# Hybrid decoder block: the mixing stage's steps one deeper, recurrence products moved from GpSimd to VectorE

## The chip, the cores and the metric

One core of one Trainium2 chip (trn2). The metric is the device time of one execution in microseconds, here the median of three runs. One core has five engines that run side by side, each with its own queue in program order: TensorE (PE in the rows, its weight loads PEld), VectorE (DVE), ScalarE (ACT), GpSimd (POOL) and SyncE (SP, which here only issues transfers). They wait for one another by semaphores.

## The reference, cut to what matters

One sequence of 512 tokens, width 1024, float32. The stage that changes is the mixer, between an input projection and an output projection:

```python
proj = h @ w_in                                # 3584 columns: aq, ak, av | hq, hf, hi, hg
# four heads of differential attention (two softmaxes of 64-wide queries and keys each)
s = einsum(q, k) * scale; p = softmax(where(causal, s, -inf))
ao = rmsnorm((p[:, :, 0] - lam * p[:, :, 1]) @ v, g_diff_sub) * (1.0 - lam_init)
# four heads of HGRN2: S_t = diag(f_t) S_{t-1} + k_t v_t^T, o_t = S_t^T q_t, k = 1 - f
ho = rmsnorm(hgrn2(silu(hq), 1 - f, hi, log f), g_hgrn_out) * silu(hg)
y = concatenate([ao, ho]) @ w_out
```

Behind it come a norm, a residual and a product-key expert layer (16384 experts, top 16 of 8 heads), which the change does not touch.

## The kernel before, in words

The program is a row of stages, each a block that all engines leave together: `stage_project`, `stage_mix`, `stage_join`, then selection, gates and experts. The large matmuls split each float32 operand into a high and a low part (`PASSES`, three products each) and stream weights in units of 128 x 1024.

**Projection** (L383 to L606). 16 column units give `projT` (queries, keys and the recurrence's q and f, turned), then three groups of four row units give `projN` (av, hg, hi). TensorE is busy nearly all the time. Between units VectorE also multiplies the conditioning vector into `w_ada` (`ada_dve`, L300), a pair of chunks at a time, due at the units in `PAIR_UNIT`. The partial sums in `acc` are added over partitions by 32 small products with a column of ones (`sum_partitions`, L312), later, in the mixing stage. SyncE's queue loads units and pairs in one written order (L447 to L472).

**Mixing** (L624 to L1006). The order is written out by hand for each engine as steps n = 0 to 17; the steps 0 to 15 are one head and one block of 128 queries each, head n // 4 and block t = n % 4, which sees k = 128 (t + 1) keys. In step n:

- TensorE makes the scores of step n into banks 0 to 3 (L943, and the causal mask by L946), then `mixedT` times v of step n - 2 (L955), then four of the 32 sums of `acc` (steps 0 to 7) or the matmuls of two level units (steps 8 to 17, L930), then turns `mixed` of step n - 1 (L973), for which it waits on VectorE.
- VectorE takes the row maxima of step n (two L840, then L842), then combines the two softmaxes of step n - 1 into `mixed` (L850 to L854, which wait for ScalarE), then in steps 1, 3, 5, 7, 9 and 11 an item of the recurrence (a subtraction of 128 x 2048: L862, L866 or L875), and in steps 8 to 17 two masked copies (L830).
- ScalarE takes the exponentials of step n (L768, waiting for `mixed` of step n - 1, because `prob` has one buffer for the pair), then copies, squares, and the exponentials of the item (L788 to L800).
- GpSimd first builds the masks (L704 to L720), then multiplies the item's exponentials with q and k into F (L725 to L742), then the norm weights into hg (L743).

The recurrence inside a chunk of 128 tokens is a sum over five levels (`LEVELS`); a level has four heads, a head is one unit of four 128 x 128 matmuls, so there are 20 units, two to a step. The first product of levels 3 and 4 reuses F's slots.

When the steps are over, TensorE turns the last product (`kbT`, L982), multiplies it with hi (L990), VectorE carries the state (L894 to L900), and TensorE forms the output of the four blocks (L1001, L1004) in banks 4 to 7. Two norms follow: GpSimd multiplies the attention rows with inverse norm and weight (L749, L751); for the recurrence VectorE copies the bank to `cat` (L907), ScalarE squares it (L809), VectorE sums (L903), ScalarE takes one root for all blocks (L811), and VectorE and GpSimd multiply the rows by the inverse norm and by hg (L693, L695).

```python
                    if n >= 2:
                        pe.wait_ge(probs_ready, 2 * (n - 1))
...
                if 1 <= n <= STEPS_A:
                    o = n - 1
                    pe.wait_ge(mixed_ready, o + 1)
```

The first wait stands ahead of the scores of step n, the second ahead of TensorE's last work of step n.

**Join** (L1011 on) turns `cat` (L1197), copies each of its eight pieces (L1084) and takes the low part (L1131), then multiplies with `w_out` (L1189).

Of the kernel before, what the change touches and what calls it, by code (L numbers as in the profile page):

```python
# [5 lines left out]
F32 = mybir.dt.float32  # L6
# [7 lines left out]
P = 128  # L14
# [70 lines left out]
def build(nc, a):  # L85
    with ExitStack() as outer:
# [27 lines left out]
        m.rows = sb("rows", [P, TT, D])  # L114

# [115 lines left out]
def row_units_pe(nc, pe, m, hl, n0, e0, groups, piece_lo=None):  # L231


    def body(g, first):
        for u in range(RAW):
            pe.wait_ge(m.unit_lo, g * RAW + (n0 + 1 + u))
            if piece_lo is not None and first:
                pe.wait_ge(piece_lo, 2 * u + 2)
# [11 lines left out]
    with pe.Fori(1, groups) as g:  # L250
        body(g, False)
# [131 lines left out]
def stage_project(nc, a, m):  # L383
# [6 lines left out]
    m.lb = m.sb("lb", [P, 2, HEADS], F32, m.keep)  # L390
    m.ada_landed = [m.sem(f"ada_landed{i}") for i in range(ADA_SLOTS)]
# [6 lines left out]
    with ExitStack() as own:  # L398
# [28 lines left out]
        first_summed = m.sem("first_summed")  # L427
# [3 lines left out]
        def _(sp):  # L431
# [31 lines left out]
            sp.dma_start(m.small[:], a.small).then_inc(small_landed, 16)  # L463
            sp.wait_ge(m.ada_dved, 1)
# [11 lines left out]
        def _(pool):  # L476
# [8 lines left out]
            m.pool.then(pool, nc.gpsimd.memset(restart[:], 1.0))  # L485
            nc.gpsimd.memset(restart[:].rearrange("p (n c) -> p n c", c=CHUNK)[:, :, 0:1], 0.0
                             ).then_inc(restart_ready, 1)
# [38 lines left out]
        def _(dve):  # L526
# [37 lines left out]
            dve.wait_ge(small_landed, 16)  # L564
# [19 lines left out]
            dve.wait_ge(m.ada_dved, len(PAIRS_FIRST) + len(PAIRS_LATER))  # L584

        @block.tensor
        def _(pe):
# [16 lines left out]
            row_units_pe(nc, pe, m, hl, 16, 16, 3)  # L604
# [19 lines left out]
def stage_mix(nc, a, m):  # L624
    with ExitStack() as own:
# [19 lines left out]
        masks = sb("masks", [P, len(LEVELS), P])  # L645
        negmask = sb("negmask", [P, P], BF16)
# [10 lines left out]
        g_diff = small[:, 4 * QK + 2 * HEADS:4 * QK + 2 * HEADS + HD]  # L657
        g_hgrn = small[:, 4 * QK + 2 * HEADS + HD:]

        masks_ready = m.sem("masks_ready")  # L660
        mod_summed, mod_read = m.sem("mod_summed"), m.sem("mod_read")
        hg_ready = m.sem("hg_ready")
# [20 lines left out]
        hgrn_read = m.sem("hgrn_read")  # L683
        squares = m.sem("squares")
        sums = m.sem("sums")
        roots, inverses = m.sem("roots"), m.sem("inverse_norms")

        hgv = hg.rearrange("p (t n) -> p t n", t=TT)

        def norm_recurrence(engine, eng, step, t):  # L690

# [10 lines left out]
        def _(pool):  # L702
# [24 lines left out]
            for level in range(1, len(LEVELS)):  # L727
                h = LEVELS[level]
                pool.wait_ge(exp_ready, level + 1)
                if level == 3:  # L730
                    pool.wait_ge(level_done, HEADS)
# [1493 lines left out]
```

## Time and profile before

| | us |
|---|---|
| runs before: median of 3 (lowest, highest) | 1940.55 (1937.95, 1943.77) |
| the profiled execution: its own time | 1938.18 |
| its span, first to last instruction | 1936.5 |
| projection, to the last of L271 | 215.2 |
| mixing, first VectorE instruction to the end of L695 | 215.5 to 367.1 |
| join and what follows | 367.6 to 1936.5 |

PE is busy for 93% of the span, DVE for 61%, ACT for 36%, POOL for 34%; the mean granted clock of TensorE is 0.949 of 2.4 GHz. In a row of instructions the first number is the start or the place, then time in us, engine, line, operation, `output<-input`, shape and count; what stands in brackets is the idle time before it and what ended it. A matmul of float32 stands as two records, one per pass.

### The profile page before, as it was taken

Reading aid. Unit: us, or ns where it says so; the run is one execution under the profiler, and the core shown is the slowest. Engines: PE = TensorE matmul, PEld = TensorE weight load, DVE = VectorE, ACT = ScalarE, POOL = GpSimd, SP = SyncE. Lnnn points to the kernel's source line nnn. Section 1 sums busy time; section 2 is a strip of 40 time slices with the busy share of each in tenths; the row PEclk is TensorE's granted clock in tenths of the full one; section 3 lists DMA queues with packets and bytes.
Section 4 is the critical chain, followed back from the end, with each engine's and each line's share of the span. In section 5 each row is a group of like instructions: output and inputs, shape, how many; then the busy total and the mean of one; then the engine's idle time right before and its main releaser. Section 6 shows DMA issues by size and latency. Waiting matters only on the chain. (4 is left out here: it accounts for less than half of the span.)

```text
span 1936.5 us, 23196 instructions
## 1 busy us (share of the span) xinstructions
PE 1791.5 (93%) x8309; PEld 1483.0 (77%) x8309; DVE 1181.0 (61%) x2034; ACT 701.1 (36%) x1107; POOL 666.5 (34%) x500
## 2 busy tenths in 40 slices
PE   7999796788998689999998999999899999999996
PEld 7777564667777578888887888888688888888885
DVE  3767467755999844554453333333367877778876
ACT  2313342352232245555553222223233333333332
POOL 0000334502777532222221000000256776667750
PEclk8999767898999899999999999999899999999998
DMA  8553000322223234645657655555488988899885
GB/s 326 212 219 118 1 1 1 131 88 98 76 69 121 82 130 149 198 159 188 195 162 223 218 181 174 178 189 179 172 287 295 351 319 322 321 339 351 326 298 198
DMA packets 159708, 369.92 MB, mean 191 GB/s; under 512 B 16288, under 2 KB 78240, under 8 KB 156192
## 3 DMA queue, kind: packets, MB, share of 16 engines
q1 hardware_dynamic: 137120, 302.08, 44.9%
q0 software_dynamic: 22528, 67.19, 9.7%
q8 instruction: 20, 0.33, 0.1%
q14 instruction: 40, 0.33, 0.1%
HBM read 306.30 MB, written 62.91 MB: 191 GB/s over the span
## 5 line engine op out<-in xcount | busy, mean ns | idle before, releaser
L2158 PE MATMUL bank<-hl,actT 128*128 128x512 f32 x2304 | 525.9, 391 | 8.9 <-DVE actT L2098 8.9
L2158 PEld LDWEIGHTS bank<-hl,actT 128*128 128x128 f32 x2304 | 434.1, 189 | 100.7 <-DVE hl L2093 9.7
L1882 PE MATMUL bank<-actT,hl 128*128 128x512 f32 x1440 | 329.5, 392 | 7.1 <-DVE hl L1853 6.8
L1882 PEld LDWEIGHTS bank<-actT,hl 128*128 128x128 f32 x1440 | 272.0, 189 | 64.3 <-DVE hl L1853 7.0
L1738 PE MATMUL bank<-actT,hl 128*128 128x512 f32 x1152 | 275.0, 395 | 6.4 <-DVE hl L1697 6.4
L1738 PEld LDWEIGHTS bank<-actT,hl 128*128 128x128 f32 x1152 | 213.9, 189 | 48.7 <-DVE hl L1697 6.7
L1518 PE MATMUL bank<-actT,hl 128*128 128x512 f32 x864 | 213.9, 408 | 38.2 <-POOL hl L1364 27.0
L2055 ACT ACTIVATE hl<-v_raw 128x1024 fp32r<-128x1024 f32 x128 | 135.6, 1060 | 286.1 <-PE bank L2158 255.2
L2014 POOL DMA_INDIRECT rows<-in_v,own_index x65 | 81.7, 1257 | 424.7 <-POOLq L1778 352.2
L1518 PEld LDWEIGHTS bank<-actT,hl 128*128 128x128 f32 x864 | 168.1, 197 | 77.7 <-POOL hl L1364 17.2
L2093 DVE TENSOR_TENSOR hl<-v_raw,hl 128x1024 fp32r<-128x1024 f32 x128 | 156.9, 1226 | 91.7 <-ACT hl L2055 91.2
L2020 POOL DMA_INDIRECT own_act<-early_activations,own_at x128 | 177.5, 1387 | 39.1 <-issue 39.1
L1636 POOL TENSOR_TENSOR onehot<-first_hits,slotsT 128x512 f32<-128x512 bf16 x48 | 91.2, 1900 | 261.0 <-DVE first_hits L1704 261.0
L1862 DVE TENSOR_TENSOR kept_acts<-kept_acts,group_gates 128x384 f32<-128x384 f32 x60 | 33.5, 558 | 171.5 <-ACT kept_acts L1836 124.1
L1364 POOL TENSOR_TENSOR hl<-raw,hl 128x1024 fp32r<-128x1024 f32 x32 | 86.9, 2714 | 83.5 <-ACT hl L1384 83.5
L1665 ACT ACTIVATE onehot<-first_hits,slotsT 128x128 f32<-128x128 bf16 x192 | 85.1, 514 | 78.4 <-DVE first_hits L1704 78.4
L1697 DVE TENSOR_TENSOR hl<-raw,hl 128x1024 fp32r<-128x1024 f32 x48 | 58.8, 1226 | 88.2 <-ACT hl L1651 88.2
L1853 DVE TENSOR_TENSOR hl<-raw,hl 128x1024 fp32r<-128x1024 f32 x60 | 73.3, 1226 | 59.1 <-ACT hl L1827 59.1
L1836 ACT ACTIVATE kept_acts<-bank 128x512 f32<-128x512 f32 x60 | 35.9, 598 | 197.5 <-PE bank L1882 197.5
L2014 POOL DMA_INDIRECT raw<-in_v,own_index x63 | 77.1, 1223 | 59.5 <-DVE raw L2114 27.5
L1754 PEld LDWEIGHTS bank<-onehot 128*128 128x128 f32 x768 | 93.1, 191 | 3.7
L1754 PE MATMUL bank<-onehot 128*128 128x128 f32 x768 | 93.4, 275 | 0.0
(257 smaller groups left out, 2271.2 us busy)
## 6 DMA issues: line engine op xcount, KB each, us to landing
raw<-in_u SPq DMA_DIRECT2D x128, 512.0 KB, 3.8
v_raw<-in_v SPq DMA_DIRECT2D x128, 512.0 KB, 6.1
expert_gates<-gates SPq DMA_DIRECT2D x12, 2048.0 KB, 9.8
group_gates<-expert_gates SPq DMA_DIRECT2D x32, 768.0 KB, 5.9
acts_in<-early_activations SPq DMA_DIRECT2D x100, 192.0 KB, 5.0
wada<-in_w_ada SPq DMA_DIRECT2D x9, 2048.0 KB, 7.6
early_activations<-kept_acts SPq DMA_DIRECT2D x60, 256.0 KB, 2.1
early_activations<-gate_acts SPq DMA_DIRECT2D x48, 256.0 KB, 2.3
```

What stands on the lines that cost most here:

```text
L1364: g.tensor_tensor(hl[:, 1, u % m.split, :], raw[:, u, :], hl[:, 0, u % m.split, :].bitcast(F32), ALU.subtract).then_inc(m.unit_lo, 1)
L1518: last = nc.tensor.matmul(m.psum[u % 2][:], hl[:, x, u % m.split, kc * P:(kc + 1) * P], m.actT[:, z, kc, :], start=(kc == 0 and j == 0), s ...
L1636: nc.gpsimd.tensor_tensor(onehot1[:, b % BUFS, 0:pool_n, :].rearrange("p t k -> p k t"), hits[:, b % BUFS, :, 0:pool_n], slotsT[:, 2, n].u ...
L1665: last = A(onehot1[:, r % BUFS, u, :], hits[:, r % BUFS, :, u], ACT.Copy, scale=slotsT[:, 2, at:at + 1])
L1738: last = nc.tensor.matmul(m.psum[n % 2][:], hl[:, x, n % m.split, kc * P:(kc + 1) * P], m.actT[:, z, kc, :], start=(kc == 0 and j == 0), s ...
L1754: last = nc.tensor.matmul(chunk_bank(b, c)[:, k * NKEY:(k + 1) * NKEY], onehot1[:, b % BUFS, u, :], onehot2[:, b % BUFS, u, :], start=True ...
L1882: last = nc.tensor.matmul(m.psum[u % 2][:], hl[:, x, u % m.split, kc * P:(kc + 1) * P], m.actT[:, z, kc, :], start=(kc == 0 and j == 0), s ...
L2014: nc.gpsimd.indirect_dma_start(out=fetched[k % FETCH], out_offset=None, in_=rows_of_v, in_offset=bass.IndirectOffsetOnAxis(ap=m.own_index[ ...
L2020: nc.gpsimd.indirect_dma_start(out=own_act[:, k:k + 1], out_offset=None, in_=acts_of_u, in_offset=bass.IndirectOffsetOnAxis(ap=m.own_at[:, ...
L2055: A(v[:, 0, j, :], v_raw[:, j, :], ACT.Copy).then_inc(v_hi, 1)
L2093: V.tensor_tensor(v[:, 1, j, :], v_raw[:, j, :], v[:, 0, j, :].bitcast(F32), ALU.subtract).then_inc(v_lo, 1)
L2158: last = nc.tensor.matmul(bank(t, half)[:], w[:, x, j, t * P:(t + 1) * P], v[:, z, j, half * S:(half + 1) * S], start=(first and j == 0 an ...
```

## The change

It does the following.

1. **Steps one deeper.** `prob` has two buffers. ScalarE's exponentials of step n wait for `mixed` of step n - 2. TensorE turns `mixed` of step n - 2 and multiplies with v for step n - 3. There are 19 steps (0 to 18).
2. **Products on VectorE.** GpSimd keeps one memset in the stage. VectorE forms the products one step after the item, in steps 2, 4, 6, 8, 10, 12.
3. **Levels, states and outputs inside the steps.** Levels run in steps 4 to 13. The turned keys follow in steps 14 and 15, the products with hi in 15 to 17, states on VectorE in 15 to 17, and the outputs of blocks 0 to 2 in 17 and 18; they go to banks 0 to 3.
4. **Tail.** The copy to `cat` goes away: ScalarE squares from the bank, takes a root per block, and copies the bank to `cat` with the inverse norm as scale (four per block). VectorE multiplies with hg, and scales the attention rows by their inverse norm. All of it is interleaved block by block.
5. **Norm weights at the join.** `m.gsub` holds the two weight vectors as columns, loaded by two small transfers (128 partitions of 4 bytes each); ScalarE's copies of `catT` take it as scale, VectorE's low part becomes a scalar_tensor_tensor.
6. **Moved to the projection.** The masks are built by GpSimd in its first microseconds. TensorE's 32 sums stand between the units: 16 behind the column units, 8 behind row group 0, 8 behind row group 2; one VectorE addition follows.

Core of the diff:

```diff
-def row_units_pe(nc, pe, m, hl, n0, e0, groups, piece_lo=None):
+def row_units_pe(nc, pe, m, hl, n0, e0, groups, banks_free=True):
...
-                if u == 0 and not first:
+                if u == 0 and not (first and banks_free):
                     pe.wait_ge(m.unit_evac, g * TT + (e0 - TT + t + 1))
...
+            for i in range(2):
+                sp.dma_start(m.gsub[:, i:i + 1], a.small[0:1, at + i * HD:at + (i + 1) * HD].rearrange("o n -> n o")
+                             ).then_inc(small_landed, 16)
...
             row_units_dve(nc, dve, m, raw, hl, m.projN, 16, 16, 3, gates_of_recurrence, between=ada_pair)
             dve.wait_ge(m.ada_dved, len(PAIRS_FIRST) + len(PAIRS_LATER))
+            dve.wait_ge(mod_summed, 1)
+            nc.vector.tensor_tensor(m.mod[:, 16:48], m.psum[3][:, 0:32], m.bada[:, 16:48], ALU.add)
...
-            row_units_pe(nc, pe, m, hl, 16, 16, 3)
+            def sums_of_pairs(pairs):
+                pe.wait_ge(m.ada_dved, len(PAIRS_FIRST) + pairs[-1] + 1)
+                for i in pairs:
+                    for c in range(i * PAIR, (i + 1) * PAIR):
+                        last = sum_partitions(nc, m, m.psum[3][:, c:c + 1], acc[:, c, :])
+                return last
+            sums_of_pairs(range(0, 4))
+            row_units_pe(nc, pe, m, hl, 16, 16, 1)
+            sums_of_pairs(range(4, 6))
+            row_units_pe(nc, pe, m, hl, 20, 20, 2, False)
+            sums_of_pairs(range(6, 8)).then_inc(mod_summed, 1)
...
-LEVEL_AT = 8
+LAST = 3
+LEVEL_AT = 4
 LEVEL_END = LEVEL_AT + HEADS * len(LEVELS) // 2
 ITEMS = {1: 0, 3: 1, 5: 2, 7: 3, 9: 4, 11: "kb"}
+PRODUCTS = {2: 0, 4: 1, 6: 2, 8: 3, 10: 4, 12: "kb"}
+KB_AT = {14: (0, 1), 15: (2,)}
+KV_AT = {15: 0, 16: 1, 17: 2}
+OUT_AT = {17: (0,), 18: (1, 2)}
...
-        prob = sb("prob", [P, 2, S])
+        prob = sb("prob", [P, 2, 2, S])
...
-                    if n >= 1:
-                        act.wait_ge(mixed_ready, n)
+                    if n >= 2:
+                        act.wait_ge(mixed_ready, n - 1)
...
+            for t in range(TT - 1):
+                square_of_out(t)
+            root(0)
+            root(1)
+            scale_out(0)
+            root(2)
+            scale_out(1)
+            square_of_out(TT - 1)
+            scale_out(2)
+            root(TT - 1)
+            scale_out(TT - 1)
...
+            def products(level):
+                if level == 0:
+                    dve.wait_ge(exp_ready, 1)
+                    V.tensor_tensor(F[:, 0, :], E[:, 0, :], kk, ALU.mult).then_inc(f_ready, 1)
+                    V.tensor_tensor(F[:, 1, :], E[:, 1, :], q, ALU.mult).then_inc(f_ready, 1)
...
+                if n in KV_AT:
+                    carry(KV_AT[n])
+                if n in PRODUCTS:
+                    products(PRODUCTS[n])
                 item = ITEMS.get(n)
...
+            dve.wait_ge(attn_root, 1)
+            V.reciprocal(ss[:, 0], ss[:, 0]).then_inc(attn_inverse, 1)
+            dve.wait_ge(attn_inverse, 1)
+            attention_rows(0)
+            sum_squares(0)
+            attention_rows(1)
+            sum_squares(1)
+            sum_squares(2)
+            inverse(0)
+            inverse(1)
+            attention_rows(2)
+            inverse(2)
+            recurrence_rows(0)
+            attention_rows(3)
+            recurrence_rows(1)
+            sum_squares(TT - 1)
+            recurrence_rows(2)
+            inverse(TT - 1)
+            recurrence_rows(TT - 1)
...
+                for i in KB_AT.get(n, ()):
+                    turn_keys(i)
+                if n in KV_AT:
+                    keys_values(KV_AT[n])
+                for t in OUT_AT.get(n, ()):
+                    if t == 0:
+                        pe.wait_ge(probs_ready, 2 * STEPS_A)
+                    recurrence_out(t)
-                if 1 <= n <= STEPS_A:
-                    o = n - 1
+                if 2 <= n < STEPS_A + 2:
+                    o = n - 2
                     pe.wait_ge(mixed_ready, o + 1)
...
-                A(catT[:, 0, dc, :], m.psum[dc % 4][:], ACT.Copy).then_inc(cat_hi, 1)
+                A(catT[:, 0, dc, :], m.psum[dc % 4][:], ACT.Copy, scale=m.gsub[:, dc // HEADS:dc // HEADS + 1]
+                  ).then_inc(cat_hi, 1)
```

In the new order TensorE's level matmuls of step n still wait for the masked copies of step n - 1, which are VectorE's last work in that step.

## Rows read from the trace of the kernel before

**Rows 1.** Windows: us, busy PE, PEld, DVE, ACT, POOL (instructions), granted clock, DMA.

```profile
60.00:142.20 82.20, 80.21 (x355) 66.09 (x353) 55.97 (x72) 15.93 (x15) 0.00 (x0) 1.00 0.60 222
142.20:215.50 73.30, 66.82 (x288) 53.68 (x288) 44.98 (x54) 23.42 (x20) 0.03 (x1) 1.00 0.25 86
215.50:278.00 62.50, 52.20 (x168) 34.36 (x169) 35.87 (x68) 25.57 (x67) 25.47 (x25) 0.50 0.00 1
278.00:346.20 68.20, 48.52 (x266) 35.31 (x265) 50.28 (x75) 23.27 (x77) 24.13 (x7) 0.81 0.00 1
346.20:367.20 21.00, 11.81 (x102) 11.22 (x101) 17.06 (x23) 6.04 (x12) 12.97 (x10) 0.88 0.00 1
```

**Rows 2.** Waits, 215 to 368 us: who waited for whom, total, times, longest.

```profile
ACT prob L768 <- DVE mixed L854: 72.1, 14, 12.9
DVE nbias L840 <- PE bank L946: 36.5, 14, 5.2
PE bank L973 <- DVE mixed L854: 27.0, 8, 9.8
```

**Rows 3.** Timeline: VectorE beside a GpSimd product, and the same operation alone.

```profile
230.78 4.49 POOL L725 TENSOR_TENSOR F<-wada 128x2048 f32<-128x2048 f32 x1 [7.59 <-ACT wada L789]
230.86 4.70 DVE L854 SCALAR_TENSOR_TENSOR mixed<-prob,rz,mixed 128x256 f32<-128x256 f32 x1
...
264.80 0.48 DVE L854 SCALAR_TENSOR_TENSOR mixed<-prob,rz,mixed 128x256 f32<-128x256 f32 x1
```

**Rows 4.** Timeline: a step of VectorE beside no product, and a state product.

```profile
240.78 1.42 DVE L840 TENSOR_REDUCE nbias<-bank 128x1 f32<-128x512 f32 x2 [5.22 <-PE bank L946]
...
243.22 0.62 DVE L854 SCALAR_TENSOR_TENSOR mixed<-prob,rz,mixed 128x384 f32<-128x384 f32 x1
243.75 2.29 DVE L875 TENSOR_TENSOR wada<-projT 128x2048 f32<-128x2048 f32 x1
...
353.20 0.85 DVE L899 TENSOR_TENSOR state<-state,decay 128x512 f32<-128x512 f32 x1
```

**Rows 5.** Groups by form: count, busy us, mean ns, idle before.

```profile
L193 DVE TENSOR_TENSOR hl<-raw,hl 128x1024 fp32r<-128x1024 f32 x36 | 44.0, 1229 | 33.4 <-ACT hl L184 20.1 <-ACT hl L1072 10.7 <-ACT hl L500 2.5
L830 DVE COPY_PREDICATED attnT<-masks,bank 128x512 f32<-128x512 uint32 x20 | 14.0, 730 | 4.7 <-PE bank L930 4.7
L789 ACT ACTIVATE wada<-wada 128x2048 f32<-128x2048 f32 x1 | 1.9, 1909 | 0.0
```

**Rows 6.** Timeline: TensorE's scores (one of two), level units and values, at both clocks.

```profile
268.18 2.07 PE L943 MATMUL bank<-projT 64*128 64x512 f32 x2
...
277.59 3.23 PE L930 MATMUL bank<-F 128*128 128x128 f32 x16
...
283.62 1.95 PE L930 MATMUL bank<-F 128*128 128x128 f32 x16
...
316.88 0.91 PE L943 MATMUL bank<-projT 64*128 64x384 f32 x2
```

**Rows 7.** Windows, columns as in Rows 1: the granted clock around its changes.

```profile
274.00:278.00 4.00, 4.00 (x17) 3.10 (x16) 3.28 (x8) 3.94 (x10) 0.00 (x0) 0.50 0.00 0
278.00:282.00 4.00, 4.00 (x24) 3.44 (x22) 2.33 (x4) 1.81 (x9) 0.00 (x0) 0.71 0.00 0
322.00:326.00 4.00, 0.00 (x0) 0.00 (x0) 3.96 (x2) 0.00 (x0) 4.00 (x2) 0.83 0.00 0
354.00:358.00 4.00, 4.00 (x39) 4.00 (x38) 3.81 (x7) 1.71 (x3) 3.76 (x4) 1.00 0.01 4
```

**Rows 8.** Timeline: the sums at half clock, and gaps of TensorE between units.

```profile
142.19 22.05 PE L245 MATMUL bank<-hl,actT 128*128 128x512 f32 x96 [1.99 <-DVE hl L193]
165.02 5.76 PE L245 MATMUL bank<-hl,actT 128*128 128x512 f32 x24 [0.78 <-DVE projN L271]
217.91 1.81 PE L314 MATMUL bank<-ones,ada_sums 128*128 128x1 f32 x8
```

**Rows 9.** Timeline: the last VectorE instruction of the mixing stage.

```profile
366.43 0.69 DVE L695 TENSOR_TENSOR rows<-rows,projN 128x512 f32<-128x512 f32 x1
```

More of the change, by code:

```diff
@@ L249, in row_units_pe @@
     body(0, True)
-    with pe.Fori(1, groups) as g:
-        body(g, False)
+    if groups > 1:
+        with pe.Fori(1, groups) as g:
+            body(g, False)
 def row_units_dve(nc, dve, m, raw, hl, dst, n0, e0, groups, after=None, done=0, evac=None,
@@ L760, in _ @@
             A(lams[:, 2:4], lams[:, 0:2], ACT.Exp).then_inc(lam_exps, 1)
-            for n in range(STEPS_A + 2):
+            for n in range(STEPS_A + LAST):
                 if n < STEPS_A:
@@ L800, in _, with square_of_out, root, scale_out @@
                     A(e[:, :, h:], e[:, :, h:], ACT.Exp).then_inc(exp_ready, 1)
[L801 to L811 removed]
+                for i in KB_AT.get(n, ()):
+                    act.wait_ge(kb_tr, i + 1)
+                    A(kbT[:, i, :], m.psum[6 + i % 2][:], ACT.Copy).then_inc(kbT_ready, 1)
+            def square_of_out(t):
+                act.wait_ge(hgrn_out, t + 1)
+                A(E[:, 0, t * S:(t + 1) * S], m.psum[t][:], ACT.Square).then_inc(squares, 1)
+            def root(t):
+                act.wait_ge(sums, t + 1)
+                A(ss[:, 1, t, :], ss[:, 1, t, :], ACT.Sqrt, bias=m.eps[:, 0:1], scale=1.0 / HD).then_inc(roots, 1)
+            def scale_out(t):
+                act.wait_ge(inverses, t + 1)
+                for h in range(HEADS):
+                    last = A(cat[:, t, (HEADS + h) * HD:(HEADS + h + 1) * HD], m.psum[t][:, h * HD:(h + 1) * HD],
+                             ACT.Copy, scale=ss[:, 1, t, h:h + 1])
+                last.then_inc(scaled, 1)
+            A(ss[:, 0], ss[:, 0], ACT.Sqrt, bias=m.eps[:, 0:1], scale=1.0 / HD).then_inc(attn_root, 1)
+            for t in range(TT - 1):
[9 more added lines that the diff above has]
+            scale_out(TT - 1)
         @block.vector
@@ L932, in level_matmuls, with turn_keys, keys_values, recurrence_out @@
                     last.then_inc(level_done, 1)
-            for n in range(STEPS_A + 2):
+            def turn_keys(i):
+                if i == 0:
+                    pe.wait_ge(f_ready, 2 * len(LEVELS) + 2)
+                    pe.wait_ge(level_copied, HEADS * len(LEVELS))
+                if i >= 2:
+                    pe.wait_ge(kbT_ready, i - 1)
+                for h in range(HEADS):
+                    last = T.transpose(m.psum[6 + i % 2][:, h * HD:(h + 1) * HD],
+                                       F[:, 3, h * S + i * CHUNK:h * S + (i + 1) * CHUNK], m.ident[:])
+                last.then_inc(kb_tr, 1)
+            def keys_values(i):
+                pe.wait_ge(kbT_ready, min(i + 2, NCH - 1))
+                if i >= 2:
+                    pe.wait_ge(state_ready, i - 1)
+                for h in range(HEADS):
+                    last = T.matmul(m.psum[7 - i % 2][:, h * HD:(h + 1) * HD], kbT[:, i, h * HD:(h + 1) * HD],
+                                    hi[:, i, h * HD:(h + 1) * HD], start=True, stop=True)
+                last.then_inc(kv_done, 1)
+            def recurrence_out(t):
+                if t >= 1:
+                    pe.wait_ge(state_ready, t)
+                for h in range(HEADS):
+                    at = slice(h * S + t * CHUNK, h * S + (t + 1) * CHUNK)
+                    out = m.psum[t][:, h * HD:(h + 1) * HD]
+                    last = T.matmul(out, attnT[:, h, t * CHUNK:(t + 1) * CHUNK], hi[:, t, h * HD:(h + 1) * HD],
+                                    start=True, stop=(t == 0))
+                    if t >= 1:
+                        last = T.matmul(out, F[:, 2, at], state[:, t - 1, h * HD:(h + 1) * HD], start=False, stop=True)
+                last.then_inc(hgrn_out, 1)
+            for n in range(STEPS_A + LAST):
                 if n < STEPS_A:
```

265 lines of the change are left out of this document (95 added, 170 removed).

## The prediction

> **What bounds the kernel now.** I read the windows first [rows 1]. In the projection TensorE is busy for 80.2 of 82.2 us and 66.8 of 73.3 us, at full clock, so anything put into its queue there is paid, except in its gaps. In the mixing stage (215.5 to 367.1, 151.6 us) no engine is busy throughout: in its first 62.5 us VectorE works 35.9 us and TensorE runs at half clock; in the next 68.2 us VectorE works 50.3 us. The waits say why [rows 2]: VectorE stood 36.5 us ahead of its row maxima until TensorE had made the scores, TensorE stood 27.0 us ahead of its transposes until VectorE had made `mixed`, and ScalarE 72.1 us for the same. That is a ring: maxima, exponentials, `mixed`, transpose, scores of the next step. The engines take turns.
>
> A third loss hides in busy time. A combination of 128x256 that takes 0.48 us alone took 4.70 us, from 0.08 us behind the start of a 4.49 us GpSimd product and to its end [rows 3]. Nine instructions of VectorE (L842, L852, L854) are stretched so in the steps; each less its plain length (0.17, 0.35, 0.48), they lose 21.3 us. The Trainium skill ("SBUF — State Buffer", on the two sides of SBUF) says that VectorE with two SBUF inputs and GpSimd share a port pair, and that the loser blocks for the whole instruction; the trace agrees. Behind the mixing stage nothing changes but a few instructions of the join, so I leave all later stages at their times.
>
> **The change part by part.** S is the stage's first VectorE instruction; before, S is 215.5 and the stage ends at S+151.6.
>
> *VectorE's work.* A step without item costs, from the first maximum to the end of `mixed`, 3.06 us where the maxima are 512 wide [rows 4], and 2.45, 2.11 and 2.55 us for 128, 256 and 384; a group of four 10.2, sixteen 40.7. Six subtractions at 2.29 [rows 4] give 13.7. Twenty masked copies are 14.0 [rows 5]. New are the products: four of 128x2048 and eight of 128x1024. No such product ran on VectorE; the nearest row is its subtraction of two SBUF operands, 1.23 for 128x1024 [rows 5] and 2.29 for 128x2048, so 18.9. A state product of 128x512 with a broadcast took 0.85 [rows 4], which by size would give 27: that is the upper end; the lower is 18.9 itself. I take the nearer row. Three states are 3.8. Sum 91, against 86 us busy before (35.9 + 50.3): the products nearly fill what the contention leaves. So this part alone gives about 2 us; the gain must come from the 44 us that VectorE stood idle in 130.7 us of steps.
>
> *TensorE's work.* A group of four steps asks for scores (two 2.07 each plus the mask pieces for the widest, at half clock [rows 6]), values, transposes and eight level units (3.23 a pair at half clock, 1.95 at full [rows 6]). From the timeline that is 12.9 + 5.5 + 3.2 + 12.9 = 34.5 us at half clock, 8.6 a step; at full 7.4 + 3.1 + 1.8 + 7.8 = 20.1 us, 5.0 a step (the widest scores at full clock are scaled from the 384 ones, 0.91 a record pair). VectorE's level steps are 5.8, 6.4, 6.8, 6.3 us. So at full clock VectorE bounds the steps, at half clock TensorE does.
>
> *Opening, steps 0 to 4.* Scores 0 start with the stage; VectorE's `mixed` of step 0 ends at S+5.1, item 0 at 7.4, and ScalarE needs two exponentials of 1.91 [rows 5] until 11.2. VectorE has maxima 2 and `mixed` 1 until 10.0 and then waits 1.2; products to 15.8, step 3 to 21.1, step 4 with its copies to 27.5. The exponentials of step 2 stand behind item 0's on ScalarE, and the turned block 0 behind those, which holds TensorE from 8.9 to 12.9: in these steps I take its clock as low from S+9 on.
>
> *Level steps 5 to 13.* TensorE is now the fuller one and works without a gap from about S+20. Before, the clock rose at 278 to 282 after such a stretch, and fell only after it had been idle from 320 [rows 7]. I take it full from S+28 and kept, since the gaps at full clock are about 1.3 us a step. VectorE's work is 5.8 + 6.4 + 6.8 + 6.3 + 5.8 + 6.4 + 6.8 + 8.5 + 3.5 = 56.3; I add 0.5 for scores and for the last exponentials. End S+84.3. Scores of step n+1 need only TensorE's levels and transpose of step n, 1.95 + 0.5 us behind the copies, so they are there when VectorE asks.
>
> *Steps 14 to 18.* Here TensorE's queue sets the pace: scores 14 and 15, keys turned, kbT's copies on ScalarE behind its exponentials, three products with hi, and the values of 14 and 15. I walk 90.4 for scores 15, 95.5 for the last kbT, 101.0 for the last transpose, 102.8 for the last values, and 24 unit matmuls (48 records at about 0.11, since 39 records filled 4.00 us [rows 7], 5.4 us) to S+108.2.
>
> *Tail.* ScalarE: square, table load 1.28, root 0.3 to S+105.2. VectorE: 12 instructions at 0.69 and four short ones, with the waits on ScalarE's roots and its 1.1 us per scaled block: S+116.4. Before, from the last step to the end at 367.1 it was 20.9 us with one root for all [rows 1, 9]; now most of that stands beside TensorE's outputs. The stage: 151.6 - 116.4 = 35.2 us gained.
>
> *Paid back.* The 32 sums. At half clock eight records take 1.81 us [rows 8]; at full clock about 0.11 a record, so 16 sums are 3.5 us and 8 sums 1.8. They stand in gaps of 1.99 and 0.78 us [rows 8], which pays for part: +1.6, +1.0, and behind group 2 they run beside VectorE's copies, +0.2 for the addition. Sum +2.8. Bounds: 0 if later gaps take it up, +9 if a record costs 0.22 at full clock too. Their partial sums are ready: the pairs are due at units 10, 16 and 22 and asked for behind units 15, 19 and 27. Two column loads of tiny pieces pass SyncE's queue before a pair and unit 4, which is issued at 45 us and needed well behind 60: about 1 us, covered; if it were not, it is 1 us. The masks (6 us of GpSimd) go to 4 to 10 us, where VectorE starts at 13.3: nothing. Join: eight scalar_tensor_tensor for eight subtractions, 0.75 against 0.69: 0.5 us. The weights themselves leave GpSimd and cost nothing in a copy's scale.
>
> *Sum.* -35.2 + 2.8 + 0.5 = -32 on the profiled execution's 1938.2 us, so 1906. That execution lies 2.4 us under the median of the three runs; on the median it is 1908.
>
> **A rule that speaks against it.** VectorE becomes the bound of the level steps. The Trainium skill ("Perfetto Trace Analysis", optimizing Scalar/DVE operations) says that with VectorE saturated some work may be offloaded, even to GpSimd, but warns of their shared port. By the first half, keeping the products on GpSimd would spare 18.9 us; the rows price it at 21.3 us of blocking, so I go by the rows.
>
> **The rivals.**
>
> *Clock low in the level steps* (0.13). TensorE is short of work at full clock, has small gaps in every step, and the clock was 0.5 over the whole 62.5 us of [rows 1] although it was busy 52.2. Then steps 6 to 13 go at TensorE's 8.6: 69 us where I have 51, +18: 1926. Against it: it rose in the first level steps before. The Trainium skill ("TensorE: Matmul & The Clock Gate", the second failure mode) says that micro-idles between groups of matmuls let the clock oscillate; that is this case.
>
> *The overlap is partial* (0.13). The queues are in order, and the level matmuls still wait for the copies at the end of VectorE's step. If each of some 14 steps keeps 0.7 us of waiting, it is +10: 1918. This is also the case in which the deepening does not do what it says.
>
> *More than that* (0.08). TensorE now works until just before the barrier, so its clock may stay full through the opening, and steps 3 to 5 shrink by up to 7 us: 1901.
>
> *Slower or no change* (0.06 together). Half clock for the whole stage with TensorE as the only bound: 86.4 + 32.3 us in the steps, 18.7 for keys, states and outputs, some 10 of tail, 2.8 in the projection, sum 150, plus each gap in its queue. With 1.5 us of gaps it is 1938, no change; from 7 us of gaps on it is slower by over 0.3%, and with 15 us 1952. Before, it waited 27.0 for `mixed` alone [rows 2], so such gaps are real, but the clock did rise three times.
>
> **How the numbers follow.** Forecast 0.60 at 1908, then 0.13 at 1926, 0.13 at 1918, 0.08 at 1901, 0.03 no change, 0.03 slower. 0.3% (5.8 us) is about what a measurement of this kernel can tell. All but the last rival are faster by over that: 0.94, 0.03, 0.03. The range takes in 1901 with half of the clock's uncertainty below it, and the first two rivals: 1897 to 1926; the products' upper end (+8) and the sums' (+6) lie in it.
>
> **What would show it.** Right: the stage ends near S+116; L854's successor never over 0.8 us; VectorE idle in steps 6 to 13 under 1 us each; granted clock 1.0 from S+30 to S+108. Wrong: idle time ahead of the maxima of over 1 us a step with TensorE as releaser, 128x1024 products well over 1.3 us, a clock of 0.5 in the level steps, or the projection longer by over 5 us.

## The result, and the profile after

The changed kernel takes 1907.79 us (median of 4 runs, 1904.27 to 1910.94) where the kernel before takes 1940.9 beside it: ratio 0.9838, 95% interval 0.9823 to 0.9853. It is faster, within 0.3 us of the forecast. The profiled execution's own time is 1909.68, its span 1908.0, and TensorE's mean granted clock 0.959.

Windows of the changed kernel, columns as in Rows 1: the projection's second half, then the mixing stage from its start S = 218.5 to its last output of TensorE at 324.6 (its tail runs on to 331.7), then the start of the join.

```profile
145.50:218.50 73.00, 69.29 (x317) 57.12 (x316) 42.05 (x51) 23.41 (x20) 0.02 (x1) 0.99 0.21 75
218.50:246.00 27.50, 22.56 (x70) 12.40 (x70) 22.41 (x42) 14.22 (x35) 1.78 (x1) 0.57 0.00 1
246.00:304.50 58.50, 47.90 (x275) 35.73 (x276) 53.60 (x99) 27.74 (x81) 0.00 (x0) 0.88 0.00 1
304.50:324.60 20.10, 16.75 (x125) 13.91 (x123) 11.92 (x27) 12.01 (x37) 0.00 (x0) 1.00 0.00 1
332.00:341.20 9.20, 5.79 (x33) 5.50 (x33) 5.07 (x6) 6.04 (x9) 8.94 (x15) 0.69 0.90 344
```

VectorE is now busy for 53.6 of the 58.5 us of the level steps, where TensorE works 47.9: it bounds them. The stage takes 113.2 us against 151.6 [rows 1]: 38.4 gained.

Waits, 218 to 332 us, and groups of VectorE by form:

```profile
PE bank L1025 <- ACT mixedT L760: 10.0, 8, 3.6
...
PE bank L968 <- DVE attnT L829: 8.6, 6, 3.0
DVE nbias L874 <- PE bank L1016: 5.6, 4, 1.8
...
L829 DVE COPY_PREDICATED attnT<-masks,bank 128x512 f32<-128x512 uint32 x20 | 13.5, 725 | 0.6 <-PE bank L968 0.6
L853 DVE TENSOR_TENSOR F<-wada 128x1024 f32<-128x1024 f32 x4 | 4.9, 1219 | 0.0
L854 DVE TENSOR_TENSOR F<-wada,projT 128x1024 f32<-128x1024 f32 x4 | 4.9, 1218 | 0.0
L888 DVE SCALAR_TENSOR_TENSOR mixed<-prob,rz,mixed 128x512 f32<-128x512 f32 x4 | 3.0, 751 | 0.1
L837 DVE TENSOR_TENSOR F<-wada 128x2048 f32<-128x2048 f32 x1 | 2.3, 2293 | 1.4 <-ACT wada L769 1.4
L888 DVE SCALAR_TENSOR_TENSOR mixed<-prob,rz,mixed 128x256 f32<-128x256 f32 x4 | 1.9, 484 | 0.1
```

The 36.5 us ahead of the row maxima [rows 2] are 5.6. TensorE waits no longer for `mixed` but for ScalarE's copies of the turned block, 10.0 us, and for the masked copies, 8.6 us. The 128x256 combination that took 4.70 us [rows 3] takes 0.48 in the mean, and the products cost what the nearest rows said.

Timeline of TensorE: the 32 sums (two records each) in the projection, and the first instruction of the stage.

```profile
140.08 3.64 PE L314 MATMUL bank<-ones,ada_sums 128*128 128x1 f32 x32
...
167.03 1.84 PE L314 MATMUL bank<-ones,ada_sums 128*128 128x1 f32 x16
...
215.43 1.84 PE L314 MATMUL bank<-ones,ada_sums 128*128 128x1 f32 x16
218.52 0.64 PE L1013 MATMUL bank<-projT 64*128 64x128 f32 x2 [1.25 <-PEq L400]
```

The stage starts 3.0 us later than before. The records of the sums themselves are short (3.64 us for 32), but right behind the first 32 the granted clock was low for 3.4 us, with TensorE busy:

```profile
143.60:147.00 3.40, 3.40 (x9) 2.72 (x10) 3.22 (x6) 0.00 (x0) 0.00 (x0) 0.50 0.71 265
```

Behind the stage the join runs from 333.1 to 406.8, 73.7 us against 70.0 before. The stages behind the join start 31 to 32 us earlier than before; the experts' phase is 3 us longer in this execution, and 0.2 us longer than before in the second one below, so that belongs to the execution.

### The profile page after: what moved, and what is told of

The parts are those of the page before. It is cut to its first block and busy times, and to the rows that moved or that the text cites. A ratio compares the mean times of both kernels' runs of the same rounds, so it can differ in the third digit from the quotient of the medians.

```text
span 1908.0 us, 23185 instructions
## 1 busy us (share of the span) xinstructions
PE 1775.7 (93%) x8309; PEld 1473.8 (77%) x8309; DVE 1171.4 (61%) x2047; ACT 706.1 (37%) x1126; POOL 619.2 (32%) x477
## 5 line engine op out<-in xcount | busy, mean ns | idle before, releaser
L2057 POOL DMA_INDIRECT rows<-in_v,own_index x65 | 89.8, 1382 | 419.7 <-POOLq L1821 351.9
```

The source lines that it names most:

```text
L2057: nc.gpsimd.indirect_dma_start(out=fetched[k % FETCH], out_offset=None, in_=rows_of_v, in_offset=bass.IndirectOffsetOnAxis(ap=m.own_index[ ...
```

## The experiments

Each time stands against runs of the kernel before on the same chip. "Stage" is the mixing stage in the run's own profile, from its first to its last instruction on VectorE and ScalarE. It is one execution each: the same changed kernel gave 113.2 and 121.6, so a difference of some us between two stages can be of the execution. The rounds were made on different chips, so the changed kernel is compared with others by ratio too; its two rows are called its first and second series.

| run | time (lowest, highest) | ratio, 95% interval | stage |
|---|---|---|---|
| changed kernel | 1907.79 (1904.27, 1910.94) | 0.9838, 0.9823 to 0.9853 | 113.2 |
| changed kernel again | 1905.38 (1896.95, 1913.55) | 0.9815, 0.9791 to 0.9840 | 121.6 |
| before + deeper steps | 1923.19 (1921.73, 1924.17) | 0.9933, 0.9916 to 0.9949 | 138.4 |
| before + products on VectorE | 1922.13 (1919.83, 1924.39) | 0.9929, 0.9913 to 0.9946 | 134.4 |
| before + both | 1923.36 (1918.8, 1926.55) | 0.9917, 0.9899 to 0.9936 | 133.1 |
| changed, products on GpSimd | 1913.19 (1908.76, 1913.66) | 0.9872, 0.9855 to 0.9888 | 123.3 |
| changed, steps not deeper | 1908.53 (1906.43, 1912.8) | 0.9862, 0.9846 to 0.9879 | 115.9 |
| changed, levels late | 1911.27 (1908.22, 1915.18) | 0.9857, 0.9832 to 0.9882 | 115.3 |
| changed, old tail | 1908.86 (1903.53, 1912.51) | 0.9844, 0.9826 to 0.9863 | 115.0 |
| changed, sums twice | 1912.04 (1910.16, 1919.64) | 0.9863, 0.9841 to 0.9885 | 116.9 |
| changed, steps filled | 1900.88 (1899.44, 1902.46) | 0.9806, 0.9783 to 0.9830 | 110.6 |
| changed, sums fill the steps | 1899.74 (1896.61, 1907.54) | 0.9802, 0.9777 to 0.9827 | 114.4 |
| all together | 1900.21 (1896.56, 1901.8) | 0.9798, 0.9774 to 0.9822 | 113.4 |

**Products on VectorE, in the kernel before.**

```diff
+PRODUCTS = {2: 0, 4: 1, 6: 2, 10: 3, 11: 4, 14: "kb"}
...
-            g.tensor_tensor(F[:, 0, :], E[:, 0, :], kk, ALU.mult).then_inc(f_ready, 1)
...
+                    V.tensor_tensor(F[:, 0, :], E[:, 0, :], kk, ALU.mult).then_inc(f_ready, 1)
```

> The kernel before, with the recurrence products alone moved from GpSimd to VectorE (steps 2, 4, 6, 10, 11, 14; the norm weights stay on GpSimd). Theory 1 (the ring of turns between VectorE and TensorE is the loss, the contention nearly pays for the products): 21.3 us of stretching go, 18.9 us of products come, so -2 us, between -6 and +3. Theory 2 (the blocked port is the main loss and the products find room in idle time): -12 to -21 us.

14.4 us faster at the medians, inside the second theory's range and far outside the first's; the stage is 17.2 shorter. Waits and one group of this run, 215 to 352 us:

```profile
ACT prob L751 <- DVE mixed L859: 50.9, 14, 8.5
DVE nbias L845 <- PE bank L953: 19.6, 12, 3.5
PE bank L980 <- DVE mixed L859: 8.5, 10, 1.6
...
L837 DVE TENSOR_TENSOR F<-wada 128x1024 f32<-128x1024 f32 x4 | 4.9, 1218 | 0.0
```

VectorE's waits for the scores fell from 36.5 to 19.6 us, TensorE's for `mixed` from 27.0 to 8.5, with the ring as shallow as before. The products stand behind `mixed`, just where VectorE would wait for TensorE's transpose and scores: 18.9 us of work went into idle time of 36.5. So what the move takes away (the stretching) is gained, and what it adds is mostly not paid.

**Deeper steps, in the kernel before.**

```diff
-        prob = sb("prob", [P, 2, S])
+        prob = sb("prob", [P, 2, 2, S])
...
-                    if n >= 1:
-                        act.wait_ge(mixed_ready, n)
+                    if n >= 2:
+                        act.wait_ge(mixed_ready, n - 1)
```

> The kernel before, with the deeper steps alone (two buffers of prob, transposes of n - 2, values of n - 3, 19 steps); products on GpSimd, sums in steps 0 to 7, levels in 8 to 17. Theory 1: the 36.5 us that VectorE waited for scores shrink, but steps 0 to 7 stay bound by TensorE at half clock with the sums in them (58 us of work in 61 us), so -12 us, between -8 and -20. Theory 2: the blocked port stays, so -5 us or less.

13.3 us faster, as the first theory has it. The stretching stays; groups of VectorE:

```profile
L843 DVE TENSOR_SCALAR nbias<-nbias 128x2 f32<-128x2 f32 x16 | 12.5, 784 | 0.6
L855 DVE SCALAR_TENSOR_TENSOR mixed<-prob,rz,mixed 128x256 f32<-128x256 f32 x4 | 8.0, 2002 | 0.1
```

The scaling of two numbers a row, 0.17 us alone, takes 0.78 in the mean: eleven of the sixteen are plain, the longest takes 4.27.

**Both, in the kernel before.**

> The kernel before with both the deeper steps and the products on VectorE, and nothing else of the change. Alone they gave 13.3 and 14.4 us. First theory: both fill the same idle time of VectorE ahead of its maxima, so together they give what the products give plus the 3 to 5 us that the depth was worth in the changed kernel: 17 to 20 us, and VectorE's waits for the scores fall from 19.6 us to under 10. Rival: the deeper steps cut a chain of TensorE that the products leave alone, so the two add up to 25 to 28 us and the moved levels, states, outputs and the tail are worth only 5.

Neither 17 to 20 nor 25 to 28: 15.3 us at the medians, and the stage only 1.3 us shorter than with the products alone. VectorE's waits for the scores are 14.8 us, not under 10. The two edits cover largely one and the same idle time. That leaves 19.9 us of stage, down to 113.2, which neither explains; the levels' run below finds most of them.

**The changed kernel with the products on GpSimd.** GpSimd gets the body of before; nothing else moves.

> The kernel after, with the products back on GpSimd, each as soon as its exponentials are there. Theory 1: VectorE is the bound of the steps; it loses 18.9 us of products and gets about 22 us of blocking back, and a level may come late for its step: +5 us against the kernel after (0 to +9). Theory 2 (the skill's rule that a saturated VectorE is helped by moving work to GpSimd): -5 to -15 us against the kernel after.

As the first theory has it: 1913.19, a ratio 0.0034 over the changed kernel's (6.6 us), and the intervals do not meet. The stage is 10 longer than in the first profile of the changed kernel and 1.7 longer than in the second. One VectorE group:

```profile
L881 DVE TENSOR_SCALAR nbias<-nbias 128x2 f32<-128x2 f32 x16 | 11.5, 718 | 0.5
```

The stretching is back. Eleven instructions in the stage are longer than the same forms in the changed kernel, by 25.8 us in all; that is more than the 18.9 us of products that VectorE is spared, and the 6.9 between them are about what the kernel lost. The Trainium skill ("Perfetto Trace Analysis", optimizing Scalar/DVE operations) allows offloading from a saturated VectorE and warns of the shared port; here the warning decides, by 6.6 us.

**The changed kernel with steps not deeper.** One `prob` buffer, exponentials of step n wait for `mixed` of n - 1, transposes one step earlier.

> The kernel after, with the steps back to the depth of before (one buffer pair of prob, transposes of n - 1, values of n - 2, 18 steps). Theory 1: the ring is back, VectorE waits for the scores again, 1.5 to 2 us a step: +25 us against the kernel after (+15 to +32). Theory 2: it hardly matters once the products are off GpSimd: +5 us or less.

The rival was right, 5 us or less: the ratio is 0.0024 higher (4.7 us, with intervals that overlap; the medians differ by 0.7), the stage 2.7 us longer than in the first profile. TensorE waits 13.5 us for `mixed` and ScalarE 45.1, but VectorE, which bounds, only 10.5 for the scores (5.6 with the deeper steps):

```profile
ACT prob L747 <- DVE mixed L887: 45.1, 14, 6.3
PE bank L1043 <- DVE mixed L887: 13.5, 10, 2.2
DVE nbias L873 <- PE bank L1015: 10.5, 7, 3.0
```

**The changed kernel again.**

> The changed kernel itself, as the base of the runs beside it. Both theories expect 0.984 of the kernel before (0.982 to 0.9855), a mixing stage of about 113 us, and a join of 66 us with the granted clock low at its first products. If the 3 us by which the experts' phase was longer in its first profile are of that execution alone, they are not seen again.

The time agrees (the ratio lies 0.0005 under the expected range, the interval reaches into it), and the experts' phase is not longer again. But the stage of this profiled execution is 121.6 us, 8.4 longer than in the first. Up to the last copies the two are alike within 1.2 us. Then, windows of this run:

```profile
294.00:302.00 8.00, 4.93 (x26) 4.75 (x25) 7.13 (x13) 1.20 (x6) 0.00 (x0) 0.69 0.00 0
302.00:310.00 8.00, 8.00 (x26) 5.08 (x25) 2.71 (x8) 2.54 (x10) 0.00 (x0) 0.50 0.00 0
```

and of the first profile of the changed kernel, whose stage starts 0.4 us later:

```profile
294.00:302.00 8.00, 5.03 (x24) 4.26 (x23) 6.71 (x13) 1.96 (x8) 0.00 (x0) 0.59 0.00 0
302.00:310.00 8.00, 7.38 (x44) 4.78 (x43) 4.68 (x13) 3.81 (x15) 0.00 (x0) 1.00 0.00 0
```

The clock fell in the same step in both. TensorE had waited 0.6, 1.7 and 0.8 us between its matmuls and then waited some 3 us for the copies of step 12 (3.07 here, 2.97 there). Here the fall, at 297.1, lies in that wait. In the first profile it came at 293.7, 0.4 us ahead of it, so the wait of 3 us can't be its cause there; a window of the first profile:

```profile
293.00:294.00 1.00, 0.95 (x6) 0.74 (x6) 1.00 (x2) 0.28 (x2) 0.00 (x0) 0.87 0.00 0
```

What differs more is how long it stayed low: from 293.7 to 300.6 in the first, here from 297.1 to 310.7, into the steps where TensorE sets the pace and busy almost throughout, and again from 317.6 to 324.4. VectorE, with 4.68 us of work in 302 to 310 there, has 2.71 here: it waits. Timeline of TensorE of this run:

```profile
297.78 3.76 PE L968 MATMUL bank<-F 128*128 128x128 f32 x16 [3.07 <-DVE attnT L829]
...
302.32 1.65 PE L1013 MATMUL bank<-projT 64*128 64x384 f32 x2
```

**Old tail.** All from the last output's copy on as before; outputs of blocks 0 to 2 stay in the steps.

> The changed kernel with the tail of before behind its last output: VectorE copies every block to cat, one root for all blocks, GpSimd scales the attention rows and multiplies the last block. Outputs of blocks 0 to 2 stay inside the steps. First theory: the tail by blocks is worth what one root behind the fourth copy costs, 3 to 8 us, seen as a longer time from the last output product (now 7 us before the stage's end) to the stage's end. Rival: the gain at the end of the stage came from forming the outputs inside the steps, and the order of the tail is worth under 2 us.

1908.86: 3.5 us over the changed kernel's second series and 1.1 over its first at the medians, with intervals that overlap. From the last output product to the stage's end it takes 9.1 us instead of 7.2. That is the rival's price, under 2 us; the time alone does not decide. In its timeline VectorE and GpSimd again work at once, and a multiplication of 128x512 takes 1.6 us where the others take 0.69:

```profile
327.61 1.63 DVE L731 TENSOR_TENSOR rows<-rows,ss 128x512 f32<-128x512 f32 x1
329.27 0.69 DVE L733 TENSOR_TENSOR rows<-rows,projN 128x512 f32<-128x512 f32 x1
```

**Levels late.**

```diff
-LEVEL_AT = 4
+LEVEL_AT = 8
-PRODUCTS = {2: 0, 4: 1, 6: 2, 8: 3, 10: 4, 12: "kb"}
-KB_AT = {14: (0, 1), 15: (2,)}
-KV_AT = {15: 0, 16: 1, 17: 2}
-OUT_AT = {17: (0,), 18: (1, 2)}
+PRODUCTS = {2: 0, 4: 1, 6: 2, 10: 3, 11: 4, 14: "kb"}
+KB_AT = {18: (0, 1), 19: (2,)}
+KV_AT = {19: 0, 20: 1, 21: 2}
+OUT_AT = {20: (0,), 21: (1, 2)}
```

> The changed kernel with its levels in steps 8 to 17 instead of 4 to 13, the products of levels 3, 4 and of the keys at steps 10, 11 and 14, and the turned keys, states and outputs of blocks 0 to 2 behind the attention steps (18 to 21). Depth, products, tail and sums stay as changed. The kernel before with depth and products alone kept 15 us of the change's 33 to 36, the tail's order 6. First theory: what is left is mostly the place of the levels, so that keys, states and outputs run beside attention steps: a mixing stage 9 to 14 us longer than the changed one, time 0.987 to 0.990 of before. Rival: the place of the levels is worth under 5 us, and the rest is spread over masks, sums and the opening: 0.982 to 0.9845.

1911.27, ratio 0.9857: between the two ranges, and 5.9 us over the changed kernel's second series at the medians. Its stage is 2.1 us over the first profile of the changed kernel and 6.3 under the second, so the place of the levels is worth a few us, as the rival has it, and not 9 to 14. What it is good for is the comparison with "before + both", which has the same levels, depth and products but a stage of 133.1 us. The last `mixed` ends 11.8 us earlier here, measured from the first maximum, and what follows is 5.8 us shorter. Of the 11.8, 2.7 are there by step 5's maxima, 9.2 by step 7's and 9.9 by step 15's. TensorE's timeline of "before + both", step 1:

```profile
218.48 1.81 PE L314 MATMUL bank<-ones,ada_sums 128*128 128x1 f32 x8
220.22 1.22 PE L951 MATMUL bank<-projT 64*128 64x256 f32 x2
```

Eight such groups of sums stand in steps 0 to 7, at half clock, between scores that VectorE waits for; with the levels late they are gone from there. The clock rose earlier too: at 247.1 us with the levels late, at 269.6 in "before + both". The same window of the two, first of "before + both":

```profile
247.00:254.00 7.00, 7.00 (x24) 4.40 (x24) 3.77 (x6) 4.18 (x10) 0.00 (x0) 0.50 0.00 0
...
247.00:254.00 7.00, 6.45 (x29) 3.21 (x28) 6.83 (x11) 4.58 (x13) 0.00 (x0) 0.99 0.00 0
```

So most of the 9.2 us came between the maxima of steps 5 and 7, where one ran at half clock and the other mostly at full. How much is the sums' own time and how much the later rise was not taken apart. The masks, which GpSimd no longer builds in these microseconds, left with them and were not tried apart.

**Sums twice.** A second `sum_partitions` ahead of each.

> The changed kernel with each of the 32 sums between the projection's units done twice, so 64 more records on TensorE and the same result. First theory (a record costs 0.11 us at full clock, 0.23 a sum, and the gaps of the queue are already full): +5 to +7.5 us, the whole of 7.4. Rival: the projection's gaps between units cover part of it (they stood at 1.99 and 0.78 us before), so under 4 us. If it is the first, the 32 sums of the change cost about what the projection is longer by, 3 us, and half of them were covered.

The time is 6.7 us longer at the medians, in the first theory's range (by ratio 4.8 us over the first series, 9.3 over the second). In the profiled execution, the slowest of the five (7.6 us over their median), the sums cost more than expected where they were put: the projection ends 11.2 us later. TensorE's timeline of this run, and windows of it:

```profile
139.73 10.48 PE L314 MATMUL bank<-ones,ada_sums 128*128 128x1 f32 x64
...
225.28 3.86 PE L314 MATMUL bank<-ones,ada_sums 128*128 128x1 f32 x32
```

```profile
140.00:144.00 4.00, 4.00 (x35) 4.00 (x34) 3.96 (x7) 1.04 (x1) 0.00 (x0) 0.90 0.29 79
144.00:148.00 4.00, 4.00 (x21) 4.00 (x20) 3.82 (x6) 0.00 (x0) 0.00 (x0) 0.50 0.58 187
148.00:152.00 4.00, 4.00 (x16) 3.61 (x16) 0.89 (x2) 0.00 (x0) 0.00 (x0) 0.50 0.00 0
```

The first 64 records took 10.48 us and not 7.3, because the clock fell to 0.50 among them though TensorE was busy throughout, and the matmuls behind them paid as well. The last 32 took 3.86, the 0.12 a record that was expected.

**Steps filled.**

```diff
+FILL_AT = {7: 4, 8: 6, 11: 2, 12: 6, 13: 11}
...
+                if n in FILL_AT:
+                    pe.wait_ge(attn_read, n - 3)
+                    for i in range(FILL_AT[n]):
+                        T.matmul(m.psum[5][:, HD:HD + P], m.ident[:], m.ident[:], start=True, stop=True)
```

> The changed kernel with 29 idle matmuls of 128x128 on TensorE (a quarter of a us each at full clock) in steps 7, 8, 11, 12 and 13, where it otherwise stands 1.1 to 3.1 us for VectorE's copies and where its granted clock fell. Output as before. In two profiled executions of the changed kernel the clock came back after 6 us in one (stage 113.2 us) and after 16 us in the other (stage 121.6 us). First theory: the falls come with these idle stretches and are the changed kernel's spread; filled, the clock stays at 1.00 from 30 us to 105 us behind the stage's start, the stage takes 110 to 114 us, and the time is 3 to 5 us under the changed kernel's (0.979 to 0.981) with less spread. Rival: the clock falls anyway, or the idle matmuls delay scores and values as much as they save: 0.982 to 0.985.

The clock is as the first theory has it. Windows of the level steps and of the last steps, and TensorE's timeline at the place where the clock fell before:

```profile
240.00:295.00 55.00, 49.45 (x324) 37.96 (x324) 52.91 (x91) 27.77 (x82) 0.00 (x0) 0.99 0.00 1
295.00:320.00 25.00, 21.52 (x156) 17.35 (x154) 15.80 (x37) 14.12 (x45) 0.00 (x0) 1.00 0.01 1
```

```profile
289.61 2.72 PE L1022 MATMUL bank<-ident 128*128 128x128 f32 x22 [0.42 <-ACT rows L755]
292.17 0.83 PE L1030 MATMUL bank<-projN,mixedT 128*128 128x128 f32 x6
294.00 2.02 PE L969 MATMUL bank<-F 128*128 128x128 f32 x16 [1.00 <-DVE attnT L830]
```

The clock does not fall, the wait is 1.00 us instead of 3, the level matmuls take 2.02 instead of 3.76. The stage is 110.6 us, the time 4.5 us under the changed kernel's at the medians, and five runs lie within 3.0 us where six of the changed kernel span 16.6. Against the changed kernel's second series the ratio is only 0.0009 lower (1.7 us), against its first 0.0032 (6.2 us), and its interval overlaps with both. So the 4.5 is less certain than what the clock did.

**Sums fill the steps.**

```diff
+SUMS_AT = {7: (0, 4), 8: (4, 11), 11: (11, 13), 12: (13, 20), 13: (20, 32)}
...
+                if n in SUMS_AT:
+                    pe.wait_ge(attn_read, n - 3)
+                    for c in range(*SUMS_AT[n]):
+                        sum_partitions(nc, m, m.psum[5][:, HD + c:HD + c + 1], m.acc[:, c, :])
```

> The changed kernel with its 32 sums taken out of the projection and put where the run beside it has idle matmuls: 4, 7, 2, 7 and 12 of them ahead of the values of steps 7, 8, 11, 12 and 13; the addition of mod stands in VectorE's tail. First theory: the projection ends 3 us earlier, and the sums fill TensorE's idle stretches and hold the clock, as idle matmuls would: 4 to 8 us under the changed kernel, 0.9775 to 0.9805. Rival: the sums save their 3 us in the projection but their 0.11 us records do not hold the clock: 1 to 3 us, 0.980 to 0.982.

The time is the first theory's, the trace is the rival's. The stage starts at 213.8 us (216.4 to 218.5 in seven runs with the sums in the projection) but takes 114.4. The clock fell at each of the five groups of sums: 0.1 to 0.7 us behind the end of four, and within the last one; TensorE's timeline and two windows of it:

```profile
288.50 4.01 PE L314 MATMUL bank<-ones,ada_sums 128*128 128x1 f32 x24
```

```profile
286.00:290.00 4.00, 4.00 (x27) 3.10 (x27) 3.81 (x2) 1.80 (x9) 0.00 (x0) 0.93 0.00 0
290.00:294.00 4.00, 4.00 (x19) 4.00 (x20) 3.56 (x10) 1.02 (x4) 0.00 (x0) 0.50 0.01 2
```

**All together.**

> The version meant to be best: the sums filled into the steps as in the run beside it, the table of the square root loaded at step 16 by a root of a constant on ScalarE (1.28 us out of the chain of the tail), and 32 idle matmuls behind the last output, so that TensorE comes to the join without standing idle. First theory: the first less 1.3 us for the table and 1.8 us for the join's first products, which then go at full clock from their start: 0.976 to 0.979. Rival: the join waits for the first tiles of w_out and for ScalarE, and the clock falls there anyway: no better than the run without the two.

The rival: no better than its neighbour (0.9798 against 0.9802). The table does load at 310.9 us, out of the chain, and the idle matmuls do keep the clock up to the join. But the stage is only 1.0 us shorter, and the join takes 71.8 us against 70.1: its last transposes stand 2.85 us for VectorE's low parts instead. These last three versions are the fastest seen, at about 1900, though their intervals overlap with that of the changed kernel's second series.

## Why the prediction came out

**The walk held, place by place.** In the first profile the opening ended at S+28.4 (walked 27.5), the last masked copy at S+83.0 (84.3), the last values at S+100.6 (102.8), the last output at S+106.0 (108.2), the stage at S+113.2 (116.4). The kinds of term in it held too: products 1.22 and 2.29, the state product 0.69 and not 0.85, copies 0.73, wait for the exponentials 1.4 ahead of the first product (1.2). VectorE bounds the level steps, and its waits for scores in steps 5 to 13 are near nothing. The sum was -32 from -35.2, +2.8 and +0.5; the trace has -38.4, +3.0 and +3.7, so -31.7. The experts' +3.1 leaves 28.5 between the two profiled executions; the medians differ by 33.1. That the sum is met so closely is luck in part: the stage gained 3.2 us more than walked and the join lost 3.2 more than priced. And the walk met one execution of two; in the other the stage took 121.6 us against its 116.4.

**"So this part alone gives about 2 us" was wrong.** It set 21.3 us of stretching out against 18.9 us of products in, as if VectorE were the bound of the old steps too, in the same sentence that names its 44 us of idle time. Alone the move gives 14.4. And "the gain must come from" the idle time, which I tied to the deeper ring: the depth alone gives 13.3, but in the changed kernel it is worth 2.7 us of stage, and with the products already moved 1.3. The end points of the walk were right because a walk counts work and waits together; the shares given to the parts were not.

**One gain was not named.** The sums stand in the sum as a cost of 2.8 us only. What their leaving gives the opening (with the masks, and with the clock that rose earlier) is most of 11.8 us of stage, the second largest piece, against 3.0 paid in the projection. The walk had it by not listing them among TensorE's work.

**The sums' price of 2.8 came out at 3.0, but not for its reasons.** Behind the first 16 sums the next unit starts 1.4 us later than before (priced at 1.6). Then came the 3.4 us at half clock, which the forecast had at full: 1.6 more. The second group added 0.8 (priced at 1.0), and later gaps took back 0.7.

The stage by parts, in one order, each from single executions and so good to some us at best: products 17.2, depth 1.3, up to the last `mixed` (the sums and masks out of the opening, mostly) 11.8, the rest of the tail and outputs 5.8 (with rounding 17.8 for the two), levels early 2.1 in an execution whose clock fell briefly. In another order depth would stand first with 13.2.

**The clock: forecast and first rival are both partly true.** "I take it full from S+28 and kept" was wrong: it fell twice in the level steps, at 263.0 within a wait of TensorE of 1.7 us, and at 293.7 behind waits of 0.6, 1.7 and 0.8 us. What failed is the reading that the clock "fell only after it had been idle from 320": in the trace of before the clock had already fallen in the level steps, at 293.9, within a wait of 6.7 us, and stayed low to 304.2. That kernel's rows, a window and a timeline row of TensorE:

```profile
294.00:298.00 4.00, 1.27 (x3) 0.79 (x4) 3.88 (x4) 1.24 (x5) 2.39 (x2) 0.50 0.00 0
...
296.73 0.69 PE L973 MATMUL bank<-ident,mixed 128*128 128x128 f32 x2 [6.71 <-DVE mixed L854]
```

The walk came out in spite of it, because VectorE bounds most of those steps and a slower TensorE cost little (VectorE waits 0.3 us for scores in steps 5 to 13, and 1.7 ahead of the maxima of step 14). The rival priced it at +18 us for all of steps 6 to 13. Against the 110.6 us of the filled run, the stage is 2.6 us longer in one execution and 11.0 in the other. The Trainium skill ("TensorE: Matmul & The Clock Gate", the second failure mode) speaks of micro-idles that let the clock oscillate; the trace agrees, with falls among waits of 0.6 to 3.1 us, and filling five of them kept the clock at 1.00 from S+25 to S+107.

**The partial overlap** did not come: VectorE waits 5.6 us in all, 1.8 of it in step 1. TensorE is the one that waits, for ScalarE's copies (10.0 us) and for the masked ones (8.6 us).

**The join** was taken at +0.5 and came at +3.7. The code is not what it lost by: with the same join the run with the sums in the steps and the one with the sums twice took 70.1 us, before it was 70.0. (A copy with the weight as its scale takes 0.69 us instead of 0.60, so it is not free as forecast, but these two runs show no loss by it.) In the first profile of the changed kernel the first tile of `w_out` came later: ScalarE waited for it, then VectorE for ScalarE, then the last transposes 3.41 us for VectorE (1.10 before). ScalarE's timeline there, and in the run with the sums in the steps, whose join starts 3.5 us earlier:

```profile
336.54 1.06 ACT L1114 ACTIVATE hl<-raw 128x1024 fp32r<-128x1024 f32 x1 [1.87 <-DMA raw<-in_w_out]
...
331.69 1.06 ACT L1108 ACTIVATE hl<-raw 128x1024 fp32r<-128x1024 f32 x1 [0.55 <-DMA raw<-in_w_out]
```

Around that wait of 3.41 us the clock fell again, from 338.1 to 344.9, and the first 24 products took 7.50 us instead of 5.72. The idle tail ahead of the join does not explain it: TensorE stood idle for 9.3 us there before, and for 7.5 now. Keeping it busy up to the join, in the last run, left a wait of 2.85 us in the same place, and the clock fell there too. Why the first tile came later is open.

## What to carry to other kernels

An engine's added work costs what is left of it once the idle time at that very place is filled; so look where in the queue it lands before setting it against what it replaces. Two remedies for the same idle time do not add, so price each with the other in place, or walk the whole. And when a kernel's runs scatter, compare the granted clock stretch by stretch in two executions: here it fell in the same step of both, came back after 7 us in one and after 14 in the other, and the stage was 8 us longer.

## What was not expected of the hardware

- The granted clock fell while TensorE was busy: among 64 records of one-column sums in the projection (10.48 us instead of 7.3), and right behind 32 of them (3.64 us; 0.50 from 143.6 to 147.0 in the first profile). A fall of 3.4 us or more stands at that place in all seven runs with the 32 sums there. Without them TensorE is idle for 2 us instead, and the clock fell in two of six. In the steps it fell at all five groups of sums; with idle matmuls of 128x128 at the same places it stayed at 1.00.
- After a fall in the same step, the clock came back after some 7 us in one execution of the same kernel and after some 14 in another.
- The stretching of VectorE beside GpSimd hits the smallest instructions too: 0.17 us became 0.72 to 0.78 in the mean of sixteen, and up to 4.27 in one.
